# Output projection of a hybrid decoder layer by a seven-product block scheme, with low parts on VectorE

## What is computed

```python
merged = gates0 * (y_ssm @ p_ssm) + gates1 * (y_attn @ p_attn) + gates2 * (y_sc @ p_sc)
out = merged @ w_out                       # (2048 x 1024) @ (1024 x 1024)
return x + rms_norm(out, norm_post)
```

## Time and profile before

| | |
|---|---|
| device time, median of 3 runs | 2757.68 us (2756.22 to 2761.54) |
| the profiled execution's own time | 2757.93 us |
| its span | 2756.3 us |
| TensorE, VectorE, ScalarE, GpSimd busy | 97%, 55%, 43%, 54% |
| output stage, first matmul to end of span | 2570.3 to 2756.3 us |

### The profile page before, as it was taken

How to read it: one execution, slowest core, us unless ns; L and a number is a source line. 1 busy time by engine, 2 the same in 40 slices (tenths; PEclk the granted TensorE clock), 3 DMA queues, 4 the chain that set the end, 5 groups by cost and what they waited for, 6 DMA issues and landing times. The chain is left out here.

```text
span 2756.3 us, 45650 instructions
## 1 busy us (share of the span) xinstructions
PE 2671.9 (97%) x17046; PEld 2199.9 (80%) x17046; DVE 1528.7 (55%) x2475; ACT 1173.3 (43%) x2207; POOL 1486.0 (54%) x1055
## 2 busy tenths in 40 slices
PE   6999999999999999999999999999999999999998
PEld 5888888888887788888888777777788877788787
DVE  6335322599452527864332565655789886843432
ACT  6232232233223543332222556565778754522432
POOL 6777767777786877777766454454100253232000
PEclk9999999999999999999999999999999999999999
DMA  3556433333224432322234555554788578954543
GB/s 126 144 177 206 144 107 123 95 112 115 62 77 144 147 125 92 115 92 62 84 108 138 179 191 170 179 193 151 208 231 207 164 228 263 314 162 152 190 138 113
DMA packets 469469, 415.30 MB, mean 151 GB/s; under 512 B 43328, under 2 KB 414272, under 8 KB 464192
## 3 DMA queue, kind: packets, MB, share of 16 engines
q1 hardware_dynamic: 467008, 404.81, 47.7%
q0 software_dynamic: 2304, 8.39, 0.8%
HBM read 282.60 MB, written 130.55 MB: 150 GB/s over the span
## 5 line engine op out<-in xcount | busy, mean ns | idle before, releaser
L559 PE MATMUL p_acc<-h_kept,w_hi 128*128 128x512 f32 x1216 | 476.9, 392 | 8.3 <-ACT work L615 3.1
L560 PE MATMUL p_acc<-h_kept,w_hi 128*128 128x512 f32 x1216 | 474.8, 390 | 0.0
L561 PE MATMUL p_acc<-h_kept,w_lo 128*128 128x512 f32 x1216 | 474.7, 390 | 0.0
L440 POOL TENSOR_TENSOR w_lo<-p_sums,w_hi 128x512 fp32r<-128x512 f32 x300 | 387.2, 1305 | 147.9 <-ACT w_hi L655 147.9
L655 ACT ACTIVATE w_hi<-p_sums 128x512 fp32r<-128x512 f32 x300 | 189.6, 633 | 508.6 <-PE p_acc L561 477.5
L280 DVE TENSOR_TENSOR p_stage<-p_acc,work 128x512 f32<-128x512 f32 x172 | 138.3, 807 | 274.5 <-PE p_acc L561 266.1
L559 PEld LDWEIGHTS p_acc<-h_kept,w_hi 128*128 128x128 f32 x1216 | 229.1, 188 | 58.8 <-ACT work L615 3.3
L561 PEld LDWEIGHTS p_acc<-h_kept,w_lo 128*128 128x128 f32 x1216 | 229.2, 189 | 48.2
L560 PEld LDWEIGHTS p_acc<-h_kept,w_hi 128*128 128x128 f32 x1216 | 229.2, 189 | 47.0
L559 PE MATMUL p_acc<-p_ops,w_hi 128*128 128x512 f32 x608 | 237.1, 390 | 1.4 <-DVE p_ops L755 1.4
L560 PE MATMUL p_acc<-p_ops,w_hi 128*128 128x512 f32 x608 | 236.6, 389 | 0.0
(11 more groups left out here) (335 smaller groups left out, 6046.4 us busy)
## 6 DMA issues: line engine op xcount, KB each, us to landing
raw<-w_in SPq DMA_DIRECT2D x100, 512.0 KB, 4.7
work<-s_gates SPq DMA_DIRECT2D x48, 512.0 KB, 7.2
p_rawb<-w_in SPq DMA_DIRECT2D x38, 512.0 KB, 3.7
keep<-w_in SPq DMA_DIRECT2D x38, 512.0 KB, 4.9
s_xbc<-p_stage SPq DMA_DIRECT2D x32, 512.0 KB, 2.6
work<-s_xbc SPq DMA_DIRECT2D x16, 1024.0 KB, 6.3
att_all<-s_att SPq DMA_DIRECT2D x24, 528.0 KB, 5.3
s_gates<-p_stage SPq DMA_DIRECT2D x24, 512.0 KB, 6.2
```

The source lines that it names most:

```text
L440: tt(w_lo[:, k], weight(u, k), w_hi[:, k], ALU.subtract).then_inc(w_made, 1)
L559: pe.matmul(bank, hi, ops[k][:, 0, c], start=c == 0, stop=False)
L560: pe.matmul(bank, hi, ops[k][:, 1, c], start=False, stop=False)
L561: last = pe.matmul(bank, lo, ops[k][:, 0, c], start=False, stop=c == 3)
```

## The change

The output projection is done by the seven-product scheme on pairs of tiles (256 tokens): per pair 7 products of 12 matmuls, each 128 tokens x 512 inputs x 512 outputs, where two plain tiles have 96 matmuls. The rows of `merged` are now the side whose 4 sums are made for each pair (GpSimd), and `w_out` is the side whose combinations are made once (VectorE), so seven 128 x 2048 operands of weights are split, in place of eight 128 x 1024 row blocks. All seven low parts of a pair's rows are made by VectorE, and so are the seven sums of products, which also carry the result into SBUF. The norm then reads SBUF. The rows of a pair come in one load of 1 MB, into two buffers that share memory with raw weight blocks. Stores of the output move from GpSimd's queue to SP's.

In the merging stage, what is prepared for the next one changes:

```diff
@@ merge_branches_stage, sync
+                        else:
                             sp.wait_ge(w_made, UNITS)
-                            for c in range(W_SPLIT, W_AHEAD):
-                                sp.dma_start(ow_raw[c], w["w_out"][...]).then_inc(out_ahead[1 + c], 16)
+                            load_block(sp, w, o_raw[1], 1, 1, o["b_loaded"][B22])
...
                         elif k:
+                            sp.wait_ge(o["op"], 1)
+                            sp.dma_start(m_raw[0], merged_tokens(d, 0)).then_inc(o["m_loaded"][0], 16)
                             break
...
-                sp.dma_start(g_t..., d["merged"][:, :, :P]...).then_inc(out_ahead[0], 16)
                 sp.wait_ge(turned, SECOND - FULL + LATE + 1)
-                for c in range(W_SPLIT):
-                    sp.dma_start(ow_raw[c], w["w_out"][...]).then_inc(out_ahead[1 + c], 16)
+                load_block(sp, w, o_raw[0], 0, 0, o["b_loaded"][B11])
+                load_block(sp, w, o_raw[2], 0, 1, o["b_loaded"][B12])
@@ gpsimd, last of the stage
+                pool.wait_ge(o["m_hi"], 1)
+                tt(m_op[0][1], m_block(m_raw[0], 0, 0), m_op[0][0].bitcast(F32), ALU.subtract).then_inc(o["m_by_dve"], 1)
@@ scalar, last of the stage (in place of m_hi and three blocks of weights)
+                act.wait_ge(o["b_loaded"][B11], 64)
+                copy(o_hi[0], o_raw[0]).then_inc(o["op_hi"], 1)
+                act.wait_ge(o["t_made"], 2)
+                for k in (1, 2):
+                    copy(o_hi[k], o_raw[k]).then_inc(o["op_hi"], 1)
+                act.wait_ge(o["m_loaded"][0], 16)
+                copy(m_op[0][0], m_block(m_raw[0], 0, 0)).then_inc(o["m_hi"], 1)
@@ vector, unit 19
+                tt(b12, b12, b11, ALU.subtract).then_inc(o["t_made"], 1)
...
+                tt(b22, b22, b12, ALU.subtract).then_inc(o["t_made"], 1)
                 gate_lane(0, use_of(0, u))
+                lo_of_operand(0)
                 gate_lane(1, use_of(1, u))
                 add_first(use_of(1, u), 1, UNITS // 2 - 1)
+                lo_of_operand(1)
```

`load_block` issues four DMAs of 256 KB; `m_raw[0]` lies in the memory of `o_raw[0]`, `m_raw[1]` in that of `o_raw[2]`, which is also `o_raw[5]`. The output stage, new (its waits that matter are kept):

```diff
@@ output_stage
+        o_raw = o_raw + [y_even..., work[:, 1], o_raw[2], o_raw[1]]
+        bank_of = [X, R0, R1, W, X, R0, W]
+        weight_of = [(0, 0), 1, 0, 2, (0, 1), 3, (1, 1)]
...
+            def _(sp):
+                def load_m(u):
+                    if u == 1:
+                        sp.wait_ge(op_ready, 6)
+                    else:
+                        for k in (PRODUCTS - 1, PRODUCTS - 2):
+                            wait_low(sp, u - 2, k)
+                    sp.dma_start(m_raw[u % 2], merged_tokens(d, u)).then_inc(m_loaded[u % 2], 16)
...
+                load_block(sp, w, o_raw[3], 0, 0, again_loaded[0])
+                sp.wait_ge(last_summed, 2)
+                load_block(sp, w, o_raw[4], 1, 0, again_loaded[1])
+                sp.wait_ge(op_ready, 3)
+                load_block(sp, w, o_raw[5], 1, 1, again_loaded[2])
...
+                load_m(1)
+                load_x(0)
+                for u in range(PAIRS):
+                    if u + 2 < PAIRS:
+                        load_m(u + 2)
+                    if u:
+                        store(u - 1)
+                        load_x(u)
...
+            def _(pool):
+                for u in range(PAIRS):
+                    wait_m(pool, u)
+                    if u:
+                        for k in (2, 1, 3, 5):
+                            wait_low(pool, u - 1, k)
...                       # sums 0 to 3, each after the one before
+            def _(act):
+                for k in range(1, 4):
+                    m_hi(0, k)
+                hi_of(3, t_made, 3)
+                hi_of(4, again_loaded[1], 64)
+                hi_of(5, again_loaded[2], 64)
+                hi_of(6, t_made, 4)
+                for k in range(4, PRODUCTS):
+                    m_hi(0, k)
+                for u in range(PAIRS):
+                    product_one(u)               # p1 <- X after product 0
+                    for k in range(PRODUCTS):
+                        if u + 1 < PAIRS:
+                            m_hi(u + 1, k)       # after product k of pair u
+                        if u and k == 0:
+                            square(u - 1)
...
+            def _(dve):
+                tt(last_gate, b_acc[:, 2], last_gate, ALU.mult)...
+                tt(total_odd[:], total_odd[:], last_gate, ALU.add)...
+                lows(0, (1, 2))
+                lo_of(2)
+                lows(0, (3,))
+                dve.wait_ge(again_loaded[0], 64)
+                tt(o_raw[3], o_raw[3], o_raw[1], ALU.subtract).then_inc(t_made, 1)
+                lo_of(3)
+                dve.wait_ge(again_loaded[1], 64)
+                tt(o_raw[6], o_raw[4], o_raw[6], ALU.subtract).then_inc(t_made, 1)
+                for u in range(PAIRS):
+                    dve.wait_ge(prod, first + 2)
+                    dve.wait_ge(p1_made, u + 1)
+                    tt(t_sum, R0, p1, ALU.add).then_inc(mixed, 1)
+                    if u == 0:
+                        lo_of(4)
+                    else:
+                        lows(u, (6,))
+                        lows(u + 1, (0,))
+                    dve.wait_ge(prod, first + 3)
+                    tt(u_sum, R1, t_sum, ALU.add).then_inc(mixed, 1)
+                    if u == 0:
+                        lo_of(5)
+                        lows(0, (4, 5))
+                        lo_of(6)
+                        lows(0, (6,))
+                        lows(1, (0,))
+                    else:
+                        finish(u - 1, 0)
+                        finish(u - 1, 1)
+                    lows(u + 1, (1, 2))
+                    dve.wait_ge(prod, first + 4)
+                    sum_to(u, 1, 1, W, u_sum)
+                    tt(t_sum, W, t_sum, ALU.add).then_inc(mixed, 1)
+                    lows(u + 1, (3,))
...                       # sum, lows 4, sum, lows 5, sum
+                finish(PAIRS - 1, 0)
+                finish(PAIRS - 1, 1)
...
+            def _(pe):
+                    for k in range(PRODUCTS):
+                        if u == 0:
+                            pe.wait_ge(op_ready, k + 1)
+                        wait_low(pe, u, k)
...
+                        if k == 6:
+                            pe.wait_ge(mixed, SUMS * u + 4)
```

More of the change, by code:

```diff
@@ L2264, in output_stage, with merged_tokens, load_block @@
-def output_stage(nc, w, d, out, eps, raw, y_lo, work, spare, split, att_all, total_odd, b_acc, total_stored, out_ahead,
-                 parts):
+def merged_tokens(d, u):
+    return d["merged"][:, :, u * 2 * P:(u + 1) * 2 * P].rearrange("b p t -> p b t")
+def load_block(sp, w, to, rows, cols, loaded):
+    for c in range(4):
+        sp.dma_start(to[:, c * BANK:(c + 1) * BANK],
+                     w["w_out"][0, rows * BANK + c * P:rows * BANK + (c + 1) * P, cols * BANK:(cols + 1) * BANK]
+                     ).then_inc(loaded, 16)
@@ L2267, in output_stage, with by_part @@
+def by_part(op):
+    return [op[:, part * BANK:(part + 1) * BANK].rearrange("p (c n) -> p c n", n=P) for part in range(2)]
+LOW_BY_DVE = (0, 1, 2, 3, 4, 5, 6)
+LOW_BY_POOL = tuple(k for k in range(PRODUCTS) if k not in LOW_BY_DVE)
+def output_stage(nc, w, d, out, eps, work, total_odd, b_acc, total_stored, o, o_raw, o_hi, o_lo, m_raw, m_op):
+    PAIRS = TILES // 2
     with ExitStack() as stack:
         s = Scope(nc, stack)
-        w_hi, w_raw, m_raw, m_hi, m_lo = output_buffers(raw, work, spare, split, att_all)
@@ new lines, in output_stage, with weight, wait_m, wait_low @@
+        again_loaded, y_stored = s.sems("o_again_loaded", 3), s.sems("o_y_stored", 2)
+        def weight(u, k):
+            which = weight_of[k]
+            return sums[:, which] if isinstance(which, int) else m_block(m_raw[u % 2], *which)
+        def wait_m(eng, u):
+            eng.wait_ge(m_loaded[u % 2], 16 * (u // 2 + 1))
+        def wait_low(eng, u, k):
+            for by, made in ((LOW_BY_DVE, m_by_dve), (LOW_BY_POOL, m_by_pool)):
+                if k in by:
+                    eng.wait_ge(made, len(by) * u + by.index(k) + 1)
@@ L2287, in output_stage, with low, wait_totals @@
+        def low(eng, u, k, made):
+            eng.wait_ge(m_hi_made, PRODUCTS * u + k + 1)
+            eng.tensor_tensor(m_op[k][1], weight(u, k), m_op[k][0].bitcast(F32), ALU.subtract).then_inc(made, 1)
+        def wait_totals(eng, slots):
+            for k in slots:
+                eng.wait_ge(total_stored[k], 16 * (20 // 2) + 16)
         with nc.Block() as block:
@@ L2341, in _ @@
[L2341 to L2350 removed]
+                copy = lambda to, of: act.activation(to, of, ACT.Copy)
```

333 lines of the change are left out of this document (176 added, 157 removed).

## The result

The kernel after takes 2768.29 us (median of 5 runs, 2763.62 to 2774.05), the one before 2757.68 (5 runs, 2754.58 to 2761.54): a ratio of 1.0033 over all runs (the two medians alone would give 1.0038), with a 95% interval of 1.0021 to 1.0045, so it is slower, by 10.6 us on the medians. Its profiled execution took 2767.12 us, 9.2 us above the one before, with a span of 2765.4, 9.1 us above. The forecast was +11.7 us and 2769.4. (One of nine executions of a later experiment, `e10_clock24`, ran with the clock at 0.65 throughout and took 4039 us; what set it off stays open, and it is left out there.)

What follows compares the result with a forecast made beforehand. The prediction took TensorE, busy 50 of 50 us in the output stage, as the bound. Its terms, -21.8 - 2.1 (old gaps) + 3.7 + 3.8 + 28.1 + 0 = +11.7, gave 2769.4 us, range 2758 to 2780.

Steps and rivals of the forecast that it cites:

- 96 matmuls less: Output stage on TensorE: 96 fewer matmuls at 0.2267 us each, -21.8 us.
- The steady pair: Pairs 1 to 6: product 6 waits 0.46 us for VectorE's sum, plus 0.15 in the restart; +3.7 us.
- The barrier: Ahead of the output stage: the first tile's load waits for shared memory, first matmul at 2574.1; +3.8 us.
- The first pair: Pair 0: gaps 21.7, half clock 5.6, restarts 0.8; 47.1 us where a steady pair takes 19.04, +28.1 us.
- I charge 1.4 us for each wait of that size or more: TensorE in pair 0: matmuls run at half clock after waits of about 3.16 us or more; four times, 5.6 us.
- the first rival: Cheaper entry: no lock between engines, load takes 4.0 us, clock holds, links short; 2757 to 2764 us, chance 0.16.
- The exclusion of the two engines: VectorE and GpSimd exclude each other, instruction by instruction; without it the first pair takes 5.2 us less.
- The tail: Behind the last matmul: later norm and SP's store, taken as 9.8 us as before, between -1 and +2.
- The faster one: Rival: pair 0's long waits ahead of products 4 and 6 hidden, 2751 us, or 2743 with more gaps gone; chance 0.12.
- The cheaper entry: The same as the first rival: nothing changes measurably, 2757 to 2764 us, if all its conditions hold; chance 0.16.
- VectorE would fall behind in every pair: Rival: GpSimd's four sums meet the chain of norms in each pair, +15 us, 2784 us; chance 0.10.
- The 84 matmuls a pair: Rival: the change doesn't reach its 84 matmuls a pair, by other operand shapes; excluded by the code.

Runs made afterwards that it cites:

- e10_clock24: As e9_sum_clock, with 24 matmuls whose result nobody reads ahead of product 4 in place of 13; ratio 0.9979 to the kernel before.
- e3_lows_late: Against the changed kernel: from pair 1 on, VectorE makes the next pair's low parts 1 and 2 after product 3's sums; 2764.78 us, ratio 1.0016.
- e5_clock: Against the changed kernel: TensorE runs unread matmuls at the merging stage's end and ahead of the first pair's products 3, 4 and 6; 2763.37 us, ratio 1.0017.
- e7_all3: Against the changed kernel: ScalarE copies pair 0's product 0 earlier, VectorE makes sums of products 3 and 4 before next-pair low parts; 2752.02 us, ratio 0.9976.
- e4_pool_extra: Against the changed kernel: three more GpSimd subtractions of SBUF tiles per pair in pairs 1 to 6, beside VectorE's norms; one execution, 2794.53 us.
- e2_w_first: Against the changed kernel: in pair 0 VectorE makes product 3's two sums before low parts 0 to 2 of pair 1; 2765.80 us, ratio 1.0017.
- e11_clock24_again: The same kernel as e10_clock24, run again without any edit; 2752.8 us, ratio 0.9969.
- e9_sum_clock: As e7_all3, with pair 0's product 5 sum right behind the first low part, and 16 and 13 unread matmuls ahead of products 3 and 4; 2754.02 us, ratio 0.9973.

## Why the prediction was right

The sign, the size and the case were right, and so was the mechanism: a first pair that is slow by the order of the work on ScalarE and VectorE, and a short wait in each steady one. The closeness of the number is partly luck. Single executions of the kernel spread over 10 us, the interval of the ratio stands for 6 to 12 us, and some terms were off in opposite directions. By its steps:

- **96 matmuls less**, -21.8, and the old gaps, -2.1: as said.
- **The steady pair**, +3.7: 0.42 us of wait for 0.46, 0.68 per pair for 0.61, so +4.1. Right, and `e3_lows_late` removed it by the one order that the sum had named. The terms of its chain as they are written add up to 8.7 and not to 8.6; the trace has 8.6 from the end of product 2 (the record that ends at 2627.09) to product 6 (2635.67). VectorE's total of 14.2 us would be 13.9 by its terms; nothing hangs on it.
- **The barrier**, +3.8: too dear. The first matmul came at 2571.88 for 2574.1, 1.6 us later than before. The load was issued at 2564.28 for 2565.1, and took 5.1 us for 5.9 up to the copy that waited for it; GpSimd's low part ended at 2571.4, and the barrier took 0.5 for 0.9:

```profile
2569.42 0.63 ACT L1988 ACTIVATE spare<-att_all 128x512 fp32r<-128x512 f32 x1 [3.88 <-DMA att_all<-s_merged]
```

The Trainium skill's rate with its fixed cost (SBUF — State Buffer, the summary; DMA: Bandwidth & Descriptors, Anatomy of one DMA) had given an estimate of 4.9 us for this load, with a fixed cost that the page states for GpSimd's way of issuing, where this load was issued by SyncE: the trace, 5.1 us, agrees with it better than with my row. The eight issues ahead of unit 18's gates cost nothing, as said: the last matmul of the merging stage started at 2568.47, where it had at 2568.95. From there to the first matmul it is 3.4 us for 1.3, so the barrier itself cost 2.1. In the profiles of the experiments that leave it alone TensorE's wait there is between 2.75 and 4.09 us (3.03 here, 0.94 before).

- **The first pair**, +28.1: 46.8 us for 47.1. The waits were 0.56, 4.06, 8.14 and 4.78, 17.5 us for 21.7: product 1 had none, and product 6's was 4.8 for 6.6, since the load took 5.2 us and the meetings with GpSimd fell more kindly. The half clock was the other way round. I had charged 1.4 us for each of four waits, 5.6. From product to product it was 2.8 in product 0 (5.53 us for 2.72), 1.6 in product 3, 2.1 in product 4 and 2.5 in product 6 (5.26 for 2.72): 9.0. Restarts and the rest were 1.2 for 0.8.

  **The term that was mis-sized** is "I charge 1.4 us for each wait of that size or more". Most of that error could not reach the time: a half clock ahead of a wait that another engine ends is hidden in that wait. The sum had its times right in this: each gap was counted from the end of a product at half clock, so a longer product would have made a shorter gap, and nothing was counted twice. The pair's length then hangs on two figures, when product 6 starts and how long it takes. It started 41.5 us behind the first matmul for 42.8 (43.7 - 0.9), and took 5.3 us for 4.1 (2.72 + 1.4). That the two errors, 1.3 too much and 1.1 too little, cancel is luck. `e5_clock` shows that product 6's 2.5 us were on the path and those of products 0 and 3 were not. What was wrong in form is the price in the first rival, 1.4 us less for each wait that does not drop the clock: for products 0 and 3 it would have been nothing, and by the chain for product 4 too.
- **The exclusion of the two engines** was right. Around the start of the stage, timelines of GpSimd and VectorE:

```profile
2573.08 2.28 POOL L2415 TENSOR_TENSOR o_sums<-o_sums,att_all 128x512 f32<-128x512 f32 x1
```

```profile
2576.05 1.22 DVE L2351 TENSOR_TENSOR spare<-o_sums,spare 128x512 fp32r<-128x512 f32 x1 [1.83 <-ACT spare L2426]
2577.18 1.76 DVE L2351 TENSOR_TENSOR o_m<-o_sums,o_m 128x512 fp32r<-128x512 f32 x1
```

Low parts take 1.22 and 1.76 us beside a GpSimd sum, 0.68 alone. With the narrower rule of the Trainium skill (SBUF — State Buffer, Who interferes with whom), that sums which read PSUM go free, the trace agrees in one place, a timeline of VectorE and one of GpSimd:

```profile
2618.88 0.69 DVE L2488 TENSOR_TENSOR o_y<-b_acc,work 128x512 f32<-128x512 f32 x1 [2.65 <-PE b_acc L2586]
```

```profile
2617.76 1.27 POOL L2415 TENSOR_TENSOR o_sums<-o_sums,att_all 128x512 f32<-128x512 f32 x1
2619.11 1.29 POOL L2417 TENSOR_TENSOR o_sums<-att_all 128x512 f32<-128x512 f32 x1
```

None of the three is longer than alone, though the VectorE sum falls almost wholly beside GpSimd's.

- **The tail**, 0: -0.5, but by two moves that cancel: the second tile's norm behind the first's made the way to the last addition 1.8 us longer (6.2 for 4.4), and from there to the end of the span, with SyncE issuing the store, it was 2.3 less (3.1 for 5.4). I had named both and priced neither.
- **The rivals.** The faster one had named the right place: bank W and product 4 in pair 0, with 2751 us if both waits were hidden. `e7_all3` gives 2752.0, but this is not quite that case: it takes product 6's wait away and leaves 3.10 us of product 4's, and 4 of its 16 us come from the steady pairs. The cheaper entry failed on most of its conditions: the two loads took 5.1 and 5.2 us and not 4.0, GpSimd and VectorE did hold each other up, and the clock dropped in four products. That VectorE would fall behind in every pair did not come about, but `e4_pool_extra` shows how near it is: three GpSimd operations in the wrong place cost 3.8 us per pair, 2.2 of them by the engines' turns and 1.6 by the clock. The 84 matmuls a pair are confirmed by the 19.04 us of `e3_lows_late`.

Summed from the trace: -21.8 - 2.1 + 4.1 + 1.6 (the first matmul) + 27.7 - 0.5 = +9.0, against 9.1 in the spans. Not tried was the barrier itself, a first tile with memory of its own; the trace alone prices it, at 3.4 us from the last matmul of one stage to the first of the next, where 1.3 were before.

## What to carry to other kernels

Fewer products pay only if the first set can be entered: here 8 sets saved 21.8 us, and the entry of the first one cost 28. The amount of work that each engine has told little here (VectorE was busy for 41.5 of 60 us in the steady pairs); what counted was each engine's order, read as "what stands ahead of the instruction that frees the next buffer", and moving a few of them turned +0.33% into -0.24%. When you move one, look at once at the next release that it now stands in front of: that took half of the gain of `e2_w_first`.

## What I had not expected of the hardware

- The half clock after a wait lasted longer than I had read, and its length did not follow the wait's: after 8.14 us the matmuls were at half clock for about 4 us, after 4.78 for all of product 6, 5.3 us:

```profile
2602.00:2603.00 1.00, 1.00 (x4) 0.81 (x3) 1.00 (x1) 0.00 (x0) 0.00 (x0) 0.50 0.95 261
```

This is the busy time of one microsecond in product 4; the clock is the third number from the end. In `e7_all3` the first five matmuls behind the barrier came at full clock and the other seven at half, so the fall can also come a microsecond behind the restart. Behind that same barrier, with waits of 2.75 to 4.09 us, the clock was at half from the first matmul in four of eleven profiles (waits of 2.93 to 4.09 us) and not in the other seven (2.75 to 3.94); what decides stays open.
- Idle time that TensorE filled with matmuls kept the clock where little or nothing was left open: none behind 24 of them in `e11_clock24_again`, 0.59 and 1.11 us ahead of products 3 and 6 in `e5_clock`. With 2.59 us left open behind 13 (`e9_sum_clock`) and 2.39 behind 32 (`e5_clock`) the half clock came back.
